# Unscaled input transposed, 0.75 MB more held ahead, half a gather behind three products, last rows added by bank

## The reference, cut to what matters

```
xn     = x * rsqrt(mean(x*x) + eps) * g_mix                 # rows of 272 tokens
proj   = xn @ w_in                                          # q, k, v, forget, latents, index keys, gates
h      = x + mixer(proj)                                    # forgetting attention, sparse latent attention, gates, w_out
hn     = h * rsqrt(mean(h*h) + eps) * g_ffn
logits = hn @ w_router + b_router ; top 4 of 32 experts, softmax over the four
for each expert e: act = swiglu(hn[rows of e] @ w_gate_up[e] + b_gate_up[e])
                   h  += gate * (act @ w_down[e] + b_down[e])
out    = rms_norm(h) without the meta tokens
```

## Time and profile before

| what | value |
|---|---|
| median of 3 runs | 1151.28 us (1150.3 to 1153.18) |
| profiled execution, own time | 1151.11 us |
| its span, first to last instruction | 1149.3 us |
| PE / DVE / ACT / POOL busy | 1094.0 / 335.1 / 214.6 / 14.7 us |
| DMA moved | 433.73 MB, mean 377 GB/s |
| expert weights in a full stage | 432 GB/s |
| mean granted TensorE clock | 0.992 |

### The profile page before, as it was taken

The page is one execution under the profiler, slowest core; times in us unless marked ns, Lnnn a source line. Parts: engine busy times, 40 slices in busy tenths (PEclk is TensorE's granted clock), DMA queues, the critical chain, the costliest instruction groups (busy, mean ns, idle before and its releaser), DMA issues. The chain is left out here.

```text
span 1149.3 us, 13558 instructions
## 1 busy us (share of the span) xinstructions
PE 1094.0 (95%) x5456; PEld 518.1 (45%) x5456; DVE 335.1 (29%) x809; ACT 214.6 (19%) x391; POOL 14.7 (1%) x28
## 2 busy tenths in 40 slices
PE   9999999999999999999989898989999989999997
PEld 6868888454343434333433343334343434343433
DVE  2285553122313222222222213131322231222223
ACT  2438781031101111111110101010111100111012
POOL 3010000000000000000000000000000000000000
PEclk9999999999999999999999999999999989999999
DMA  9914228879999999999999999999999999999995
GB/s 307 287 38 147 76 108 345 368 279 435 426 435 427 432 435 429 432 435 428 433 435 428 433 435 428 432 436 428 431 432 413 433 428 433 432 425 428 427 418 239
DMA packets 39866, 433.73 MB, mean 377 GB/s; under 512 B 3144, under 2 KB 19938, under 8 KB 24340
## 3 DMA queue, kind: packets, MB, share of 16 engines
q1 hardware_dynamic: 38464, 430.11, 89.5%
q0 software_dynamic: 960, 2.30, 0.6%
q10 hardware_dynamic: 404, 0.79, 0.2%
HBM read 432.13 MB, written 1.05 MB: 377 GB/s over the span
## 5 line engine op out<-in xcount | busy, mean ns | idle before, releaser
L1870 PE MATMUL psum<-arena 128*64 128x512 f32 x1016 | 225.8, 598 | 7.4 <-DMA arena<-in_w_gate_up 7.4
L1870 PE MATMUL psum<-ring,arena 128*64 128x512 f32 x968 | 215.6, 600 | 6.3 <-DMA ring<-in_w_gate_up 6.3
L1870 PEld LDWEIGHTS psum<-arena 128*64 128x64 f32 x1016 | 71.0, 137 | 154.6 <-issue 140.4
L1887 PE MATMUL psum<-ring,arena 128*64 128x512 f32 x544 | 122.9, 602 | 13.7 <-DMA ring<-in_w_down 13.7
L1870 PEld LDWEIGHTS psum<-ring,arena 128*64 128x64 f32 x968 | 67.6, 138 | 146.9 <-issue 134.9
L1294 DVE TENSOR_TENSOR arena<-psum,biasT 128x512 f32<-128x512 f32 x64 | 44.3, 692 | 295.9 <-PE psum L1825 292.0
L947 DVE TENSOR_TENSOR arena<-psum,vT 128x512 f32<-128x512 f32 (+2 forms) x43 | 28.5, 669 | 334.3 <-PE psum L1752 325.3
L1887 PE MATMUL psum<-arena 128*64 128x512 f32 x480 | 108.0, 602 | 14.5 <-DMA arena<-in_w_down 14.5
L856 ACT ACTIVATE arena<-psum 128x1024 f32<-128x1024 f32 x32 | 32.7, 1023 | 316.6 <-PE psum L1870 301.7
L1318 DVE TENSOR_TENSOR h<-h,psum 128x1024 f32<-128x1024 f32 x64 | 75.3, 1218 | 21.2 <-PE psum L1912 19.2
L1887 PEld LDWEIGHTS psum<-ring,arena 128*64 128x64 f32 x544 | 41.2, 138 | 85.0 <-issue 79.1
(11 more groups left out here) (243 smaller groups left out, 763.7 us busy)
## 6 DMA issues: line engine op xcount, KB each, us to landing
arena<-in_w_gate_up SPq DMA_DIRECT2D x28, 4096.0 KB, 28.5
ring<-in_w_gate_up SPq DMA_DIRECT2D x25, 4096.0 KB, 29.8
ring<-in_w_down SPq DMA_DIRECT2D x14, 4096.0 KB, 28.0
arena<-in_w_down SPq DMA_DIRECT2D x13, 4096.0 KB, 30.1
ring<-in_w_gate_up SPq DMA_DIRECT2D x9, 2048.0 KB, 26.8
ring<-in_w_in SPq DMA_DIRECT2D x14, 1024.0 KB, 12.3
arena<-in_w_gate_up SPq DMA_DIRECT2D x6, 2048.0 KB, 24.7
arena<-in_w_gate_up SPq DMA_DIRECT2D x8, 1024.0 KB, 30.0
```

What stands on the lines that cost most here:

```text
L1870: ins = mm(bank[home + n][h * CAP:(h + 1) * CAP, :], xg[:, c, e * CAP:(e + 1) * CAP], part, start=c == 0, stop=c == CH - 1)
L1887: ins = mm(bank[home][n * CAP:(n + 1) * CAP, :], rows[:, c * CAP:(c + 1) * CAP], w[:, n * 512:(n + 1) * 512], start=first, stop=last)
```

## The change

The diff has four parts.

1. Input: TensorE transposes the rows of the two token tiles as they were loaded. The features go into `xr` (the place of `kcat`, free until later) with their gain, and `mid_block` multiplies those. The row scale comes in afterwards: ACT's copy of `mid` takes it per row, and for the features TensorE lays it along the partitions of a bank (`scale_along`, a product with the identity) and DVE multiplies `xr` with it into `xnT` (`scaled_features`), which the keys wait for. The meta tokens stay as they were. One warm-up product fewer.
2. Held ahead: the first 1536 columns of the last chunk of the first expert's second slot (0.75 MiB) don't lie in the slot but in `gl` and `yr`, loaded after the router's products (`stash`). Their place in the slot gets that part of the slot's next content at once (`second_load`), so `first_refill` has that much less to load.
3. The second half of the first gather's second tile stands behind chunk c = 2 of the first products. The next two-column step of the rank table moves from ahead of the pass count into the pass.
4. The last expert's rows are added in four steps of one bank. TensorE ends the last pass with half a gather less.

```diff
+STASH = D + 512
...
-WARM_UP = 3
+WARM_UP = 2
...
+        xr = kcat[:, 0:CH * SEQ].rearrange("p (c k) -> p c k", c=CH)
...
+            def second_load():
+
+                c0 = (QUARTERS - 1) * QWIDTH
+                for a, z in ((0, c0), (c0 + STASH, EWIDTH)):
+                    sp.dma_start(eslot(1)[:, a:z], gate_up_rows(0, 1)[:, a:z]).then_inc(s_rest, 16)
+                sp.dma_start(eslot(1)[:, c0:c0 + STASH],
+                             rows_of(ESLOT + 1 - GU_LOADS, 1)[:, c0:c0 + STASH]).then_inc(wide_loaded[1], 16)
+
+            def stash():
+
+                c0 = (QUARTERS - 1) * QWIDTH
+                sp.dma_start(gl, gate_up_rows(0, 1)[:, c0:c0 + D]).then_inc(s_stash, 16)
+                sp.dma_start(yr, gate_up_rows(0, 1)[:, c0 + D:c0 + STASH]).then_inc(s_stash, 16)
...
+                        if n == 1 and q == QUARTERS:
+                            rows, c0 = rows_of(idx - GU_LOADS, 1), (QUARTERS - 1) * QWIDTH
+                            sp.wait_ge(wide_used[1], base + q - 1)
+                            part_of(idx, rows, q - 2, q - 1, part_loaded[1])
+                            sp.wait_ge(wide_used[1], base + q)
+                            sp.dma_start(eslot(idx)[:, c0 + STASH:EWIDTH],
+                                         rows[:, c0 + STASH:EWIDTH]).then_inc(wide_loaded[1], 16)
...
-            for idx in range(2):
-                sp.dma_start(eslot(idx), gate_up_rows(0, idx)).then_inc(wide_loaded[idx], 16)
+            sp.dma_start(eslot(0), gate_up_rows(0, 0)).then_inc(wide_loaded[0], 16)
+            second_load()
...
+            sp.wait_ge(s_rt, 2)
+            stash()
             whole_pass(0)
...
-                copy_out(("mid", t), mid[:, t, :], job_bank(("mid", t))[:, 0:MID])
+                sc.wait_ge(s_xri, t + 1)
+                wait_filled(sc, ("mid", t))
+                empty_end(sc.activation(mid[:, t, :], job_bank(("mid", t))[:, 0:MID], ACT.Copy,
+                                        scale=st[:, 3 + t:4 + t]), ("mid", t))
...
-                link(v.reciprocal(st[:, 3 + t:4 + t], st[:, 3 + t:4 + t]))
-                src = h1[:, t * D:(t + 1) * D] if t < 2 else xs[0:META, 2 * D:3 * D]
-                v.tensor_scalar(xs[0:rows, t * D:(t + 1) * D], src, st[0:rows, 3 + t:4 + t], None,
-                                ALU.mult).then_inc(s_xs, 1)
+                ins = v.reciprocal(st[:, 3 + t:4 + t], st[:, 3 + t:4 + t])
+                if t < 2:
+                    ins.then_inc(s_xri, 1)
+                    return
+                link(ins)
+                meta_rows = xs[0:rows, t * D:(t + 1) * D]
...
-                    empty_end(scaled(xnT[:, 4 * n:4 * n + cs, col:col + rows], src,
+                    dst = xr[:, 4 * n:4 * n + cs, t * P:(t + 1) * P] if t < 2 else xnT[:, :, col:col + rows]
+                    empty_end(scaled(dst, src,
...
+            def scaled_features(t):
+
+                rows, col = TILES[t]
+                wait_emptied(dve, ("xT", t, 1))
+                dve.wait_ge(s_rb, t + 1)
+                v.tensor_tensor(xnT[:, :, col:col + rows], xr[:, :, t * P:(t + 1) * P],
+                                bank[7 - t][:, 0:P].unsqueeze(1).broadcast_to([P, CH, P]), ALU.mult).then_inc(s_xn, 1)
...
             for t in (1, 2):
                 input_scale(t)
                 input_features(t)
+                scaled_features(t - 1)
...
-            link(v.tensor_scalar(rk3[:, :, EXPERTS:RCOLS], rk3[:, :, 0:2], -float(CAP), None, ALU.add))
...
+            def add_last_rows(x, b):
+
+                for t in range(2):
+                    for n in range(2):
+                        if n == 0:
+                            dve.wait_ge(s_bank, b * 2 + (t + 1))
+                        else:
+                            dve.wait_ge(s_sc, x * 2 + (t + 1))
+                        part = h1[:, t * D + n * 512:t * D + (n + 1) * 512]
+                        ins = v.tensor_tensor(part, part, bank[4 + 2 * t + n], ALU.add)
+                    ins.then_inc(s_acc[t], 1)
+                for t in range(2):
+                    dve.wait_ge(s_acc[t], x + 1)
...
                 v.memset(st[:, 51:52], 0.0).then_inc(s_low, 1)
+                mlink(v.tensor_scalar(rk3[:, :, EXPERTS:RCOLS], rk3[:, :, 0:2], -float(CAP), None, ALU.add))
...
-                pe.wait_ge(s_xs, t + 1)
+                if t < 2:
+                    pe.wait_ge(s_x[t], 16)
+                else:
+                    pe.wait_ge(s_xs, 1)
+                tokens = h1 if t < 2 else xs
...
-                                 xs[0:rows, t * D + (4 * n + c) * P:t * D + (4 * n + c + 1) * P],
+                                 tokens[0:rows, t * D + (4 * n + c) * P:t * D + (4 * n + c + 1) * P],
...
-                    ins = mm(job_bank(name)[:, s * half:(s + 1) * half], xnT[:, c, col:col + rows],
+                    ins = mm(job_bank(name)[:, s * half:(s + 1) * half], xr[:, c, t * P:(t + 1) * P],
...
+            def scale_along(t):
+
+                pe.wait_ge(s_xri, t + 1)
+                mm(bank[7 - t][:, 0:P], st[:, 3 + t:4 + t].broadcast_to([P, P]), ident, start=True,
+                   stop=True).then_inc(s_rb, 1)
 
             input_rows(0)
             mid_block(0, 0, 0, 5)
             input_rows(1)
             mid_block(0, 0, 5, CH)
+            scale_along(0)
             mid_block(1, 0, 0, 6)
+            scale_along(1)
             input_rows(2)
             mid_block(1, 0, 6, CH)
             mid_block(0, 1)
...
             for k in range(4):
+                if k == 0:
+                    pe.wait_ge(s_xn, 2)
...
             pe.wait_ge(s_np, 1)
             n_pass = pe.value_load(npi[0:1, 0:1], min_val=1, max_val=SEQ // CAP)
-            gather_first(1, 1)
...
                         before_end()
+                    if first_pass_rows is not None and j == 0 and k == 1:
+                        pe.wait_ge(s_rest, passes[1])
+                    if first_pass_rows is not None and c == CH - 1:
+                        pe.wait_ge(s_stash, passes[1])
...
+                            if first_pass_rows is not None and c == CH - 1 and h * D + n * 512 < STASH:
+                                part = yr if h else gl[:, n * 512:(n + 1) * 512]
...
                     used(ins, idx)
+                    if c == 2 and first_pass_rows is not None:
+                        gather_first(1, 1)
...
+                        if each_bank and n == 0:
+                            ins.then_inc(s_bank, 1)
                     ins.then_inc(s_sc, 1)
...
-                scatter(x + 1, pickgT_end)
+                scatter(x + 1, pickgT_end, True)
...
-                gather(1)
+                gather_first(0, 1)
```

More of the change, by code:

```diff
@@ L326, in build @@
                           for n in range(ESLOT) for q in range(QUARTERS - 1)}
+        s_rest = sem("second_load_without_stashed_columns_loaded")
+        s_stash = sem("stashed_columns_loaded")
         s_eighth = sem("first_eighth_of_first_slot_used")
@@ L334, in build @@
         s_sd = sem("x_deviation_ready")
-        s_xs = sem("x_scaled")
+        s_xs = sem("meta_tokens_scaled")
+        s_xri = sem("x_row_scale_ready")
+        s_rb = sem("x_row_scale_along_features")
+        s_xn = sem("x_features_scaled")
         s_mss = sem("mid_squares_summed")
@@ L396, in build @@
         s_fri = sem("final_scale_ready")
+        s_bank = sem("first_bank_of_tile_holds_last_rows")
         s_fg = sem("rows_of_tile1_times_gain")
@@ L539, in first_refill @@
                             sp.dma_start(dst[:, :, 512:D], src[:, :, 512:D]).then_inc(part_loaded[0], 16)
+                            continue
+                        if n == 1 and q == QUARTERS:
[5 more added lines that the diff above has]
+                                         rows[:, c0 + STASH:EWIDTH]).then_inc(wide_loaded[1], 16)
                             continue
@@ L648, in _ @@
                         sp.wait_ge(wide_used[idx], b * (QUARTERS * PASS_USES))
-                        if idx < 3:
+                        if idx == 1:
+                            second_load()
+                        elif idx < 3:
                             sp.dma_start(eslot(idx), gate_up_rows(idx // 2, idx % 2)).then_inc(wide_loaded[idx], 16)
@@ L658, in _ @@
                         kept_pieces(n, n + 1, 0)
+                    sp.wait_ge(s_sc, b * (2 * EXPERTS))
+                    stash()
                     whole_pass(b)
@@ L963, in input_scale @@
                 dve.wait_ge(s_sd, t + 1)
-                link(v.reciprocal(st[:, 3 + t:4 + t], st[:, 3 + t:4 + t]))
-                src = h1[:, t * D:(t + 1) * D] if t < 2 else xs[0:META, 2 * D:3 * D]
-                v.tensor_scalar(xs[0:rows, t * D:(t + 1) * D], src, st[0:rows, 3 + t:4 + t], None,
-                                ALU.mult).then_inc(s_xs, 1)
+                ins = v.reciprocal(st[:, 3 + t:4 + t], st[:, 3 + t:4 + t])
[4 more added lines that the diff above has]
+                meta_rows = xs[0:rows, t * D:(t + 1) * D]
```

(20 more changed lines are left out.)

## The result

The changed kernel took 1153.68 us (median of 20 executions, 1151.75 to 1157.03), the kernel before 1151.34 (20 executions): ratio 1.0019, interval 1.0013 to 1.0026, so 1.5 to 3.0 us slower. I had forecast 1.5 us faster and a range up to 1152.8. A second set, 11 executions on another chip, gave 1.0020 (1.0011 to 1.0030). The profiled execution took 1154.66 us, its span is 1152.6; before 1151.11 and 1149.3.

The account below looks back on a forecast made before the run. Bound: first slot part's return plus bytes left to move, behind TensorE's mixer work. Gains 0.1 (input) + 1.3 (stash and gather) + 0.05 (last rows) = 1.45 us off 1151.11 give 1149.66, median 0.17 above: 1149.8; range 1147.4 to 1152.8.

Parts of the forecast that it names:

- cover of the bias loads: First expert pass: ACT's bias loads, issued at 249.6 us, land at 253.5, 2 us before c = 7 needs them.
- rival 3: Bias loads beside a full queue land at 254.9 to 258.1 us, holding c = 7 by 2.5 us: 1152.3 us; chance 0.09.
- The rule on queues: DMA engines alternate between queues by packets, so bias loads escape SP's megabytes and land about as in the old trace.
- The reserve at 293.2 us: Weight load issued at 293.2 us had 2.1 us to spare before the DMA engines ran dry, limiting the gain to 1.3.
- rival 4: Reserve at 293 us is 1 us or less, eaten by the gather's 0.8; 0.15 left: 1151.1 us; chance 0.15.
- the stash's 1.8 us: Full DMA stretch: 0.786 MB held ahead leaves 1.82 us less to move, if a slot part is always free.
- the first product comes sooner behind the gather: Start of expert part: first product waits for half a gather less; 0.35 us gain taken, between 0.1 and 0.4.
- TensorE 0.8 us later: From c = 3: half gather's 1.15 us less the 0.35 earlier start; slots handed back 0.8 us later (0.7 to 1.05).
- Input edit: Kernel start: unscaled transposes save 0.57 us, scale_along costs 0.51; 0.1 gained taken, bounds 0.2 gained to 0.3 lost.
- rival 2: Shorter warm-up leaves TensorE at 1.2 GHz beyond the DMA wait at 10.78 us: 1152.2 us; chance 0.14.
- Last rows: Kernel end: four one-bank adds start 0.43 us earlier, take 2.76 against 2.35; 0.05 us gained (0 to 0.3).
- likeliest case: The forecast itself: covers hold, the stash is cut by the reserve, 1.45 us gained, 1149.8 us; chance 0.45.

Follow-up runs that it names:

- e1: Kernel before with only the gather split (second half behind c = 2, rank step into the pass): 1153.03 us, ratio 1.0014.
- e13: Kernel before with only its two bias loads held until the first slot is used up: 1155.62 us, ratio 1.0043.
- e5: Changed kernel with the bias loads issued early, between the two gathers: 1152.61 us, ratio to the kernel before 1.0007.
- second profile: Another profiled execution of the unaltered changed kernel, router gather at its old speed: first product at 242.30 us against 244.56 in the first.
- e16: Changed kernel with three warm-up pairs in place of two, one profiled execution only: 1153.12 us, no ratio.
- e2: Kernel before with only the stash (0.75 MiB more held ahead): 1150.62 us, ratio 0.9996.
- e6: Changed kernel without the split of the gather: 1151.94 us, ratio to the kernel before 0.9998.
- e12: Changed kernel with three warm-up pairs in place of two: 1153.25 us, ratio to the kernel before 1.0013.
- e10: Changed kernel with early bias loads and the 4 MiB loads issued as halves: 1151.39 us, ratio to the kernel before 0.9995.
- e11: Changed kernel without the gather split, with the 4 MiB loads issued as halves: 1150.25 us, ratio to the kernel before 0.9988.
- e9: Kernel before with only the 4 MiB loads issued as two halves, no stash: 1151.92 us, ratio 0.9996.
- e3: Kernel before with only the input edit (rows transposed unscaled, one warm-up product fewer): 1152.07 us, ratio 1.0005.
- e8: Kernel before with the stash and five 4 MiB loads issued as halves, each released by its half slot: 1150.17 us, ratio 0.9987.
- e4: Kernel before with only the last rows added bank by bank: 1151.62 us, ratio 0.9998.
- e7: Changed kernel measured again, unaltered, beside other runs: 1153.41 us, ratio to the kernel before 1.0020.
- e14: Changed kernel with early bias loads, halved 4 MiB loads and three warm-up pairs: 1151.62 us, ratio to the kernel before 1.0001.

## Why the prediction was wrong, point by point

**The step that failed** is the cover of the bias loads: "The old ones took 3.5 us at the median: 253.5, covered by 2 us." The new time of issue was right (250.0 forecast; 251.81, in an execution that was 1.75 us late at the first product). The duration was read from a row where SP's queue was empty, and put into a stretch where it was full: 6.0 and 6.2 us in the changed kernel, 6.3 in e1, 7.0 in e13, against 2.5 in e5 at the early place. The rows that I had for a load beside a full queue (4.9 and 8.1 us, rival 3) held the answer between them; I gave that case 0.09. What it costs can be summed at the 16 instructions that follow c = 7 (256.69 us before): in the second profile the first product is 0.51 earlier and the half gather 1.09 more, which gives 257.27, and they come at 259.08: 1.8 us. The same sum gives 1.3 in the first profile (1.75 later, 1.09 more: 259.53 against 260.88), 2.0 in e1 (258.73) and, without the wait, 0.15 in e5 (258.22).

**The rule on queues** ("DMA: Bandwidth & Descriptors", Queues, rings and completion order, in the Trainium skill) says that an engine takes turns between queues by packets. The trace agrees: from 252.5 to 256.8 us q10 has 21.8% of the engines' time beside q1's 77.4%. What failed is my consequence from it, that the loads land as in the old trace: issued while SP's queue was empty they took 2.4 to 3.9 us over all profiles, beside a full one 5.7 to 7.0. Taking turns costs time, and the first turn came 3.1 us after the issue.

**The reserve at 293.2 us** was the second step that failed: "14.2 - 12.1 = 2.1". The 2.4 us fixed came from one load of 1 MiB. Six profiles with clearly more than 9.7 us between the two landings there (10.0 to 11.8) landed the 4 MiB after 12.8 (e16), 13.0 (e5, e13), 14.1 (e1), 14.2 (e2) and 14.6 us (e6): the fixed part is 3.1 to 4.9, and the reserve of the kernel before lies between 0 and 1.4, not at 2.1. That is about rival 4's condition. In the second profile the load was issued at 295.62, 2.4 later than before, and landed 1.6 later (309.0 against 307.4), and the gaps from 264.0 to 309.0 us exceed their bytes' time by 3.0: the stash's 1.8 us and what the reserve did not hold. By then it was no longer this load that ran short (9.7 behind the one before), but those ahead of it, issued at 265.3 and 268.7 (5.5 and 5.9 us for 2 MiB, whose bytes take 4.9) and at 275.6 and 282.9 (10.6 and 10.2 for 4 MiB). Two gaps do not fit a short queue, the last of these and one of 11.5 us in e12: their loads were issued 6.3 and 5.6 us before the landing ahead of them. Their cause is open.

**Right in mechanism and size:** the first product comes sooner behind the gather (242.30 is 1.08 us behind the gather's end at 241.22; before 242.81 and 241.45, 1.36), 0.28 against 0.35 taken; the half gather costs 1.16 us with its start where it was put; the stash's two loads are in no one's way (issued at 237.97 and 238.34, in the stage in which nothing moved before). The sum "TensorE 0.8 us later" is near the 0.8 us that e10 and e11 differ by.

**Input edit:** in the first profile, tile 1's transposes start at 11.03, at the DMA wait's end as forecast ("about 11.2"), the two `scale_along` take 0.40 each, and the meta rows are scaled at 15.60 (forecast 15.7). Their product begins at 16.99 where it was 17.17:

```profile
10.71 0.30 PEld L1511 LDWEIGHTS psum<-ring,arena 128*128 128x128 f32 x2 [1.63 <-DMA ring<-in_w_in]
11.03 1.00 PEld L1492 LDWEIGHTS psum<-kst,h 128*128 128x128 f32 x8
...
13.15 0.40 PEld L1519 LDWEIGHTS psum<-kst,st 128*128 128x128 f32 x2
```

One pair of profiles misleads here; all 18 say the opposite. From the start of tile 1's transposes to this product it is 5.75 or 5.76 us in the 11 profiles with the edit and 5.31 to 5.36 in the 7 without: 0.4 us more. And the transposes (their product rows) start no earlier: 11.18 to 12.06 us with the edit (mean 11.66), 11.02 to 11.90 without (11.54). The 0.57 us that the prediction wanted to save come from a profile in which TensorE waited for VectorE's scaling (0.34 us); of the other six without the edit only e9 shows that wait (0.21). So the product starts at 17.42 on the mean in place of 16.89, and the edit costs some 0.5 us where 0.1 gained was taken. The times allow it (e3: 1.0005, 0.9996 to 1.0014) but don't show it, and e11 against e8 (0.9988, 0.9987) shows nothing of it. The clock drop at the front (rival 2) occurs in e6 and e11, ten products in 4.03 us, but their transposes start at 11.90 and 11.39, inside the range of the others: the cover by `w_in` held, as the prediction had it.

**Last rows:** forecast 0.05 gained, read from the trace 0.2 lost, both below what the times can tell (e4 0.9998). Against the earlier trace rows: 

```profile
1142.53 0.22 PEld L1999 LDWEIGHTS psum<-kst,arena 64*128 64x128 f32 x2 [0.21 <-issue]
1142.82 2.48 DVE L1382 TENSOR_TENSOR h<-h,psum 128x512 f32<-128x512 f32 x4 [5.78 <-PE psum L1999]
```

The adds start 0.29 us behind that weight load, before 0.23: waiting for one bank did not bring them forward; why, the traces don't say. They take 2.48 in place of 2.35, so four of them overlap a little (4 x 0.69 would be 2.76).

**The sum.** -0.28 (first product) + 1.09 (half gather) + 1.3 to 1.8 (bias wait) + 0.2 (end), with the stash eaten: 2.3 to 2.8 us by the traces, 2.1 to 2.3 measured. The sum leaves out the input edit's 0.5 and counts nothing for the stash, of which e2 kept 0.5; its close agreement is in part luck. The likeliest case of the prediction needed all covers to hold at once; the conditions of rivals 3 and 4 both came true, and I had priced each alone. The chances of the five cases already add up to 1.00, so the mixtures, and with them the 0.81 inside the range, were not worked out.

**A version that beats both:** the kernel before with stash and halves, 1150.17 us, 0.9987 (0.9978 to 0.9996); with input edit and last rows besides 0.9988. That is 3.2 us below the changed kernel beside it (e7, 1153.41).

## What to carry to other kernels

A load's time from issue to landing belongs to the state of the queues at its issue: when a change moves a small load, take its duration from a row beside the same traffic, and put the longest such row into the likeliest case, not into a rival. A surplus of bytes held ahead is only worth what the slots' turn lets through: measure the least issue-to-landing time with a load of the same size, and where the reserve is short, split the load so that its first half is released sooner. Where TensorE's pace sets the releases, most of a delay in front of them is paid at the end (here 0.7 to 1.0 of it), so moving work from under a wait into the open needs a gain larger than the whole of it. And a gain read as the idle time ahead of one instruction in one profile is not yet a gain: in further profiles another wait may end just before it.

## What the runs showed of the hardware that was not expected

- 128 KB of bias on ACT's queue land 2.4 to 3.9 us after an issue with SP's queue empty (e14, e2) and 5.7 to 7.0 us after one with it full (e12, e13).
- A wait of 2.80 us in the midst of dense products (e13) was followed by 3 us at the lower level of TensorE's clock (0.50), which added 1.8 us to it; waits of 0.98, 1.44 and 1.65 us (changed kernel twice, e1) were not followed by a drop.
- 4 MiB issued some 3 us before the landing ahead of them take 12.8 to 14.6 us (e16, e6), 3.1 to 4.9 more than the 9.7 between landings of a full queue; 1 MiB into an idle queue 2.4 more than its bytes.
- In the router TensorE's clock fell to 0.50 for 3.5 to 7 us in 4 of 18 profiles; in the two of the changed kernel the first product then came at 244.56 and 245.04 us in place of 242.30.
